# First projection of a diffusion block: the read-out matrix (C) for latent tokens alone and not transposed, each tile's product begun with its latent columns, feature rows of x no longer stored

## What is computed

```
xbc = h @ w_in[:, x | B | C]            # 2048 + 512 + 512 = 3072 channels
xbc = silu(depthwise_conv_centred(xbc, conv_w, conv_b))     # 5 taps along the tokens
xs, bm, cm = split(xbc, [2048, 2560])
chunk_states = einsum(bm, decay_end, xdt)       # needs x and B, context and latents
lmat   = einsum("bcign,bcjgn->bcijg", cm, bm)   # C against B
y_off  = einsum("bcign,bcigr,bcgrpn->bcigrp", cm, exp(a_cum), s_prev)   # C reads the states out
q, k, v, gates, z, dt  = other columns of the same projection
```

## Time and profile before

| | |
|---|---|
| median of three executions | 2770.59 us (2769.58 to 2772.36) |
| the profiled execution | 2772.97 us, its span 2771.3 us, mean TensorE clock 0.941 |
| from the start to 81.3 us | loads, layer norm, modulation |
| convolved tiles, PE | 81.3 to 477.0 us (product 0 to turn 23) |
| q, k and gate tiles | 477.0 to 788.3 us |
| later stages | states, scan, attention, branches, residual, experts, output |

### The profile page before, as it was taken

The page is one execution under the profiler, slowest core; times in us unless marked ns, Lnnn a source line. Parts: engine busy times, 40 slices in busy tenths (PEclk is TensorE's granted clock), DMA queues, the critical chain, the costliest instruction groups (busy, mean ns, idle before and its releaser), DMA issues. The chain is left out here.

```text
span 2771.3 us, 33343 instructions
## 1 busy us (share of the span) xinstructions
PE 2470.3 (89%) x12980; PEld 2015.3 (73%) x12980; DVE 1714.2 (62%) x1827; ACT 1097.7 (40%) x1379; POOL 496.9 (18%) x405
## 2 busy tenths in 40 slices
PE   7899999999989997894899969999782799999993
PEld 2788888777779886673566649999672688888882
DVE  5555555444315664684565546674557599999996
ACT  3323323221114111453233354442332477777772
POOL 0101001012101441697000000000343011111112
PEclk8899999999999998897899989999895899999996
DMA  5333334238524784995545359978435599999994
GB/s 214 97 122 107 115 122 123 99 119 276 187 96 143 278 296 136 318 306 143 100 78 109 70 148 265 262 216 248 155 107 222 219 371 403 402 399 397 398 383 136
DMA packets 361200, 581.15 MB, mean 210 GB/s; under 512 B 24053, under 2 KB 268117, under 8 KB 337705
## 3 DMA queue, kind: packets, MB, share of 16 engines
q1 hardware_dynamic: 329050, 459.94, 49.4%
q0 software_dynamic: 26384, 111.52, 12.4%
q10 hardware_dynamic: 5632, 7.87, 1.0%
HBM read 460.35 MB, written 118.64 MB: 209 GB/s over the span
## 5 line engine op out<-in xcount | busy, mean ns | idle before, releaser
L2633 DVE TENSOR_TENSOR e_wlo<-e_w,e_whi 128x2048 fp32r<-128x2048 f32 x188 | 425.6, 2290 | 43.7 <-ACT e_whi L2582 42.3
L2582 ACT CAST e_whi<-e_w 128x2048 fp32r<-128x2048 f32 x192 | 365.4, 1910 | 125.5 <-PE e_gu L2759 84.2
L445 PE MATMUL f_lat<-h_hi,w_hi 128*128 128x512 f32 x800 | 255.2, 400 | 0.2 <-DVE w_lo L598 0.2
L445 PE MATMUL f_lat<-h_lo,w_hi 128*128 128x512 f32 x800 | 251.3, 395 | 0.0
L445 PE MATMUL f_lat<-h_hi,w_lo 128*128 128x512 f32 x800 | 251.0, 395 | 0.0
L2093 PE MATMUL b_acc<-b_hi,b_whi 128*128 128x256 f32 x768 | 218.6, 285 | 7.4 <-issue 7.4
L2093 PE MATMUL b_acc<-b_lo,b_whi 128*128 128x256 f32 x768 | 217.9, 284 | 0.0
L2093 PE MATMUL b_acc<-b_hi,b_wlo 128*128 128x256 f32 x768 | 217.9, 284 | 0.0
L445 PEld LDWEIGHTS f_lat<-h_hi,w_hi 128*128 128x128 f32 x800 | 135.9, 189 | 33.4 <-issue 7.5
L445 PEld LDWEIGHTS f_lat<-h_hi,w_lo 128*128 128x128 f32 x800 | 136.4, 188 | 27.6
L445 PEld LDWEIGHTS f_lat<-h_lo,w_hi 128*128 128x128 f32 x800 | 136.4, 188 | 27.5
(11 more groups left out here) (377 smaller groups left out, 5545.6 us busy)
## 6 DMA issues: line engine op xcount, KB each, us to landing
e_w<-in_w_gate_up SPq DMA_DIRECT2D x128, 1024.0 KB, 11.1
e_w<-in_w_down SPq DMA_DIRECT2D x64, 1024.0 KB, 9.2
w_raw<-in_w_in SPq DMA_DIRECT2D x50, 512.0 KB, 4.0
t_space<-xbcT POOLq DMA_DIRECT2D x18, 1280.0 KB, 6.6
before<-t_space SPq DMA_DIRECT2D x16, 1024.0 KB, 4.1
y_before<-before SPq DMA_DIRECT2D x64, 256.0 KB, 6.0
xbcF<-f_out POOLq DMA_DIRECT2D x24, 640.0 KB, 3.5
xbcT<-t_out POOLq DMA_DIRECT2D x24, 640.0 KB, 4.4
```

The source lines that it names most:

```text
L445: mm = nc.tensor.matmul(o, weights[:, b, k, :], part[:, k, a:a + n], start=(k == 0 and n_pass == 0), stop=(k == KT - 1 and n_pass == 2))
L2582: nc.scalar.copy(whi[:, slot % SPLIT], w[:, slot]).then_inc(w_hi, 1)
L2633: V.tensor_tensor(wlo[:, slot % SPLIT], w[:, slot], whi[:, slot % SPLIT].bitcast(F32), ALU.subtract).then_inc(w_split, 1)
```

## The change

1. C tiles (20 to 23): no context matmuls, no context copies, convolution over 1024 instead of 1284 columns, SiLU for the latents alone, no transposes, no `turned_copy`, no store to `xbcT`. NT = 20 is the number of tiles that are still transposed.
2. `product` begins with the three passes of k-block 0 over the latents; only then does it wait on `f_ctx_turned` and make the three context passes of k-block 0. From k-block 1 on a group is latents, then context.
3. `xbcF` is stored for B and C tiles only, and only its latent columns.
4. To treat tiles apart, the loops are shorter: PE's covers tiles up to 19, ACT's up to 17, DVE's up to 19, POOL's up to 15; the rest is written out. Counts that semaphores are compared with are adapted.

```diff
                 def product(f, b, ctx, after_turn=False):
                     pe.wait_ge(w_free, f + 3)
                     pe.wait_ge(acc_free, f + 1)
-                    if after_turn:
-                        pe.wait_ge(ctx_turned, f + 1)
-                    outs = [(cxt[:, b, 0:CTX], 0, CTX)] if ctx else []
-                    outs += [(lat[:, b, 0:512], CTX, 512), (lat[:, b, 512:1024], CTX + 512, 512)]
-                    for k in range(KT):
+                    outs = [(lat[:, b, 0:512], CTX, 512), (lat[:, b, 512:1024], CTX + 512, 512)]
+                    context = [(cxt[:, b, 0:CTX], 0, CTX)] if ctx else []
+
+                    def passes(k, outs):
                         for n_pass, (weights, part) in enumerate(((whi, hi), (whi, lo), (wlo, hi))):
...
+                    passes(0, outs)
+                    if after_turn:
+                        pe.wait_ge(ctx_turned, f + 1)
+                    if ctx:
+                        passes(0, context)
+                    for k in range(1, KT):
+                        mm = passes(k, outs + context)
                     mm.then_inc(used, 1)
...
-                with pe.Fori(1, NX // 2) as i:
+                with pe.Fori(1, NT // 2) as i:
                     product(2 * i, 0, True, True)
                     turn(2 * i - 1, 1)
                     product(2 * i + 1, 1, True, True)
                     turn(2 * i, 0)
-                product(NX, 0, False)
-                turn(NX - 1, 1)
-                product(NX + 1, 1, False)
+                product(NT, 0, False)
+                turn(NT - 1, 1)
+                for f in range(NT + 1, NX + 2):
+                    product(f, f % 2, False)
                 rotated(NX, 0)
...
-                        nc.scalar.copy(padded[:, b, 2:2 + CTX], cxt[:, b, 0:CTX])
+                        if not latents_only:
+                            nc.scalar.copy(padded[:, b, 2:2 + CTX], cxt[:, b, 0:CTX])
                         nc.scalar.copy(padded[:, b, 6 + CTX:6 + CTX + SEQ], lat[:, b, :]).then_inc(acc_free, 1)
-                        if not (isinstance(f, int) and f == 0):
+                        if not isinstance(f, int) or 0 < f <= NT:
                             turned_copy(f - 1, 1 - b, turn - (1 - b))
-                            act.wait_ge(wide_out[b], 16 * turn)
+                        if isinstance(f, int) and f >= NXS + 2:
+                            act.wait_ge(wide_out[b], 16 * (turn - NXS // 2))
...
+                    a = 4 + CTX if isinstance(f, int) else 0
-                    nc.vector.tensor_scalar(conv[:, b], padded[:, b, 0:W_OUT], tap[:, b, 0:1], None,
+                    nc.vector.tensor_scalar(conv[:, b, a:W_OUT], padded[:, b, a:W_OUT], tap[:, b, 0:1], None,
...
-                    pool.wait_ge(wide_made, f + 3)
-                    pool.dma_start(xbcF[rows, :], wide[:, b]).then_inc(wide_out[b], 16)
+                    if isinstance(f, int):
+                        pool.wait_ge(wide_made, f + 3)
+                        pool.dma_start(xbcF[rows, CTX:TOK], wide[:, b, CTX:TOK]).then_inc(wide_out[b], 16)
+                        if f >= NT:
+                            return
                     pool.wait_ge(tp_free, f + 2)
```

More of the change, by code:

```diff
@@ L381, in project_f_stage, with pairs @@
         wa = s.x["w_ada"][0].rearrange("(p k) n -> p k n", k=KT)
[L383 to L388, removed]
+        NXS = D_INNER // P
+        NT = NXS + GROUPS
+        def pairs(eng, f0, f1, step):
+            with eng.Fori(f0 // 2, f1 // 2) as i:
                 for b in range(2):
-                    step(2 * i + (f0 + b), b, kind, i + f0 // 2, 2 * i + (w0 + b))
+                    step(2 * i + b, b, "xbc", i, 2 * i + b)
         with nc.Block() as block:
@@ L459, in rotated @@
                     pe.wait_ge(acc_free, f + 3)
-                    pe.wait_ge(tp_free, f + 1)
+                    pe.wait_ge(tp_free, f + (NT - NX + 1))
                     for n in range(2):
@@ L530, in evacuate @@
                     if kind == "xbc":
+                        latents_only = isinstance(f, int) and f >= NT
                         act.wait_ge(conv_step, CS * f + CS)
-                        nc.scalar.copy(padded[:, b, 2:2 + CTX], cxt[:, b, 0:CTX])
+                        if not latents_only:
+                            nc.scalar.copy(padded[:, b, 2:2 + CTX], cxt[:, b, 0:CTX])
                         nc.scalar.copy(padded[:, b, 6 + CTX:6 + CTX + SEQ], lat[:, b, :]).then_inc(acc_free, 1)
-                        if not (isinstance(f, int) and f == 0):
+                        if not isinstance(f, int) or 0 < f <= NT:
                             turned_copy(f - 1, 1 - b, turn - (1 - b))
-                            act.wait_ge(wide_out[b], 16 * turn)
+                        if isinstance(f, int) and f >= NXS + 2:
+                            act.wait_ge(wide_out[b], 16 * (turn - NXS // 2))
                         act.wait_ge(conv_step, CS * f + 3 * CS)
-                        nc.scalar.activation(wide[:, b, 0:CTX], conv[:, b, 0:CTX], ACT.Silu, bias=tap[:, b, CONV_W:CS])
+                        if not latents_only:
+                            nc.scalar.activation(wide[:, b, 0:CTX], conv[:, b, 0:CTX], ACT.Silu, bias=tap[:, b, CONV_W:CS])
                         nc.scalar.activation(wide[:, b, CTX:TOK], conv[:, b, 4 + CTX:W_OUT], ACT.Silu,
@@ L542, in evacuate @@
                         if within < 2:
-                            act.wait_ge(wide_out[b], 16 * NX // 2)
+                            act.wait_ge(wide_out[b], 16 * (NX - NXS) // 2)
                         else:
@@ L570, in _ @@
                 step(1, 1, "xbc", 0, 1)
-                with act.Fori(1, NX // 2) as i:
-                    step(2 * i, 0, "xbc", i, 2 * i)
-                    step(2 * i + 1, 1, "xbc", i, 2 * i + 1)
+                pairs(act, 2, NXS + 2, step)
+                for f in range(NXS + 2, NX):
+                    step(f, f % 2, "xbc", f // 2, f)
                 split_hi(NX + 1, 1, NX // 2)
-                turned_copy(NX - 1, 1, NX // 2 - 1)
                 evacuate(NX, 0, "q", NX // 2, 0)
@@ L624, in _ @@
                 dve.wait_ge(taps_in, 16)
-                pairs(dve, "xbc", convolve)
+                pairs(dve, 0, NT, convolve)
+                for f in range(NT, NX):
+                    convolve(f, f % 2, "xbc", f // 2, f)
                 dve.wait_ge(turns_in, 32)
@@ L697, in store_split @@
                             pool.dma_start(part[rows, 0:CTX], kept[:, b, 0:CTX].bitcast(F32)).then_inc(qk_out[b], 16)
-                pairs(pool, "xbc", store)
+                pairs(pool, 0, NXS, store)
+                for f in range(NXS, NX):
+                    store(f, f % 2, "xbc", f // 2, f)
                 for n in range(NQK):
@@ L728, in _ @@
                     pool.wait_ge(qk_out[b], 16 * (NQK + NQK - NQ))
-                    pool.wait_ge(wide_out[b], 16 * NX // 2)
-                    pool.wait_ge(turned_out[b], 16 * NX // 2 + 16)
+                    pool.wait_ge(wide_out[b], 8 * (NX - NXS))
+                    pool.wait_ge(turned_out[b], 8 * NT + 16)
 class Ahead:
```

11 lines of the change are left out of this document (6 added, 5 removed).

## The result

| | before | changed |
|---|---|---|
| median | 2770.09 us (2769.58 to 2772.36, 4 runs) | 2729.62 us (2725.09 to 2730.30, 4 runs) |
| profiled execution, its span | 2772.97, 2771.3 us | 2730.19, 2728.5 us |

The ratio is 0.9849, 95% interval 0.9832 to 0.9866: 40.5 us faster. The forecast was 2734.0 with a range of 2731.5 to 2741.5, so the time lies outside the range, on the fast side.

The account below looks back on a forecast made before the run. The prediction took PE's instruction stream to bound this stage and pass its gain to all later stages. 19.5 + 6.3 + 10.8 = 36.6 us off the profiled 2772.97 gave 2736.4, as a median 2734.0, range 2731.5 to 2741.5.

Parts of the forecast that it names:

- (a): PE's wait for the context copy behind each turn: gap falls from 1.99 to 1.01 us, 20 gaps, 19.5 us gained.
- (b): Transposes of C on PE: turns 20 to 23 go, with waits and slow first groups, 6.3 us gained.
- (c): Context products of C on PE: 96 matmuls removed at 0.113 us each, 10.8 us gained.
- (d): ACT and DVE in C tiles: less work, hidden by PE; weights still ready with 0.4 us to spare, worth 0.
- (e): Stores to xbcF: 16 go and 8 shrink, on a queue that keeps up anyway, worth 0.
- (f): Loops cut short and written out: worth 0, since PE is full either way.
- R1: Rival: weights become the bound in C tiles, costing 4.9 us, 2739; chance 0.12 together with small costs of the wait.
- R2: Rival: the wait only moves to the context matmuls, so reordering gains nothing, 2753.5 us; chance 0.05.
- R3: Rival: something outside PE's stream sets the stage's end, so the gain isn't passed on, 2770.6 us; chance 0.02.
- R4: Rival: TensorE's clock falls to 1.2 GHz for tiles 20 to 25, 56 us lost, 2790; chance 0.03.

Follow-up runs that it names:

- reorder_only: The kernel before with only the new order in `product`: latent passes of k-block 0 first, then the wait; C's context and transposes stay. 2749.16 us, ratio 0.9925.
- wide_conv: The changed kernel with the convolution of C tiles over 1284 columns again, the first 260 of which nobody reads. 2731.19 us.
- before_unrolled: The kernel before with tiles 22 and 23 of PE's loop written out, no work more. 2766.15 us, ratio 0.9985.
- c_only: The changed kernel with the old `product`: context matmuls of k-block 0 and their wait come first again. 2745.04 us, ratio 0.9913.
- lead_one: The changed kernel with one latent pass (two matmuls) instead of three ahead of the wait on f_ctx_turned. 2738.03 us.

## Why the prediction was wrong where it was

The steps of the sum held. (a): 19.2 by the distances for 19.5, all 20 gaps at 1.01 us, by reorder_only and by the timeline. (b) and (c): 17.1 for 17.1, from turn 18 to product 25. The removed context matmul was 0.113 us. The Trainium skill (TensorE: Matmul & The Clock Gate, Back-to-back issue gap) has 262 cycles for it, an estimated 0.109 us, which would have given 36.2. Its sustained figure for pairs of load and matmul, 0.131 us at 512 columns, isn't borne out by this stage, where such a matmul takes 0.23 us before and after. (d): 0, the slack was 0.2 to 0.5 us where 0.4 was reckoned, and wide_conv shows the price of missing it. (e) and (f) inside the stage: 0.

The step that failed is the one ahead of the sum: that what PE's stream gains "moves the end of the stage, and with it all later stages, which start on what it leaves", one to one, and with it step (f), which priced loops cut short and written out at 0. In its place the later stages took 3.8 us less by the medians (6.1 in the two traces). before_unrolled shows 4.3 us (1.7 to 6.6) for two tiles written out and nothing else, and the traces show a part of such differences in the stretches that PE runs at the lower clock. What joins the two stays open. The range fell with it: its lower end was the forecast less the spread of three executions, 2.5 us, as though the later 1983 us could only repeat themselves. The executions of the kernel before that the ratios count reach from 2766 to 2776 us, and its medians by session from 2769.3 to 2772.9; 5 us to either side would have been honest.

Of the rivals, R1's mechanism is real, but the change stayed 0.2 us clear of it. R2's full form is c_only, and lead_one is its partial form: with a lead of one pass it would have cost 8.5 us. R3 didn't occur. Nor did R4 in its form of whole C tiles at the lower clock: from 81 to 440 us PE is never idle and the clock is 0.99, the first 6 us alone at the lower level. In the later stages, where no rival looked, the clock did move the time by some us.

## What to carry to other kernels

Where one engine's stream is full, sum start-to-start distances of whole repeats; the sum of 36.6 us met 36.5 that way, while durations and idle entries would have missed (0.28 for 0.113, 0.73 for 0.98). When a wait guards only one operand of a long product, put the matmuls that don't need it first, and count the lead against the moment at which the guard is lifted, since a lead of 0.47 us left half of a wait that 1.4 us removed. A forecast to within a few us for a long program must allow for untouched stages that take another length. The controls are a kernel with the same work and another length of code, the same kernel a second time, and the record of the granted clock laid beside the stages.

## What the hardware showed that I had not expected

The same work, with about 328 instructions more in PE's program, took 4.3 us less in the kernel before and some 3 us more in the changed one, while the stage that was rewritten kept its length (706.9 against 707.0 us, 670.4 and 670.6 against 670.5). The second was measured twice, with medians of 2732.71 and 2732.49 us, but not beside the changed kernel; the first once, 11 runs of it beside 15 of the kernel before, with an interval that ends 0.06% below no change. The granted clock changes level often in the later stages (0.50 to 0.99 by stage above), and the lengths of these stages differ by 1 to 3 us between executions of one kernel, in the states and the experts together with the time at the lower level.
